# Attention of a hybrid decoder step: ScalarE scales each item's weights by a factor that VectorE makes; GpSimd leaves the attention

## What is computed

```
# q (T, 8 heads, 64), two K/V groups of 4 heads; query block i holds 128 tokens
p_c = masked_softmax(q . kc);  o_c = p_c @ vc                 # 32 compressed blocks
p_s = masked_softmax(q . ks);  o_s = p_s @ vs                 # selected: here all causal keys
p_w = masked_softmax(q . kw);  o_w = p_w @ vw                 # window of 512 tokens
out = g[..., 0:1] * o_c + g[..., 1:2] * o_s + g[..., 2:3] * o_w   # g = sigmoid(gates), per token, head, branch
```

## Time and profile before

| | us |
|---|---|
| median of three runs | 2125.23 (2118.19 to 2125.60) |
| the profiled run | 2124.39 |
| span of its profile | 2122.2 |
| attention in it | about 462 to 850 |

### The profile page before, as it was taken

One profiled execution on the slowest core, in us unless ns is written; L12 is line 12 of the kernel. 1 busy time (PEld: TensorE's weight loads), 2 busy tenths in 40 slices (PEclk: granted clock), 3 DMA queues, 4 the chain that ended last, 5 costly groups with the idle time before them and its releaser, 6 DMA issues.

```text
span 2122.2 us, 28687 instructions
## 1 busy us (share of the span) xinstructions
PE 2029.2 (96%) x11391; PEld 1604.4 (76%) x11391; DVE 810.9 (38%) x1514; ACT 516.8 (24%) x934; POOL 389.5 (18%) x447
## 2 busy tenths in 40 slices
PE   6999999989999998999999998899999999999998
PEld 3588877775666555666676676899999999988875
DVE  2444334466665657422202256311111111235354
ACT  2322100234443444101101045311111111123232
POOL 0000111222231323221000055000000000155542
PEclk8999999989999999999999998999999999999999
DMA  9342010032000000663324354112112112235453
GB/s 362 126 157 100 21 41 21 1 97 70 11 11 11 11 10 3 179 170 108 102 59 129 111 177 139 61 40 60 40 40 60 40 40 60 87 122 168 146 188 104
DMA packets 172940, 184.89 MB, mean 87 GB/s; under 512 B 9893, under 2 KB 143117, under 8 KB 172366
## 3 DMA queue, kind: packets, MB, share of 16 engines
q1 hardware_dynamic: 172814, 183.12, 27.7%
HBM read 170.74 MB, written 16.53 MB: 88 GB/s over the span
## 4 chain that ended last, share of the span: by engine, by line
PE 87%; DVE 4%; DMA 2%; ACT 2%; issue 2%; POOL 1%; SPq 1%; ACTq 0%; POOLq 0%; DVEq 0%
PE ps L2605 23%; PE ps L2507 11%; PE ps L2110 9%; PE ps L2131 5%; PE ps L2549 5%; PE ps L2550 5%; PE ps L2551 5%; PE ps L2377 4%; PE ps L2367 3%; PE ps L2328 3%; PE ps L2345 3%; DMA arena<-in_w_ada 1%; POOL arena L1000 1%; PE ps L2070 1%; DVE arena L601 1%
## 5 line engine op out<-in xcount | busy, mean ns | idle before, releaser
L2605 PE MATMUL ps<-h_hi,wup_hi 128*128 128x344 f32 x1056 | 338.3, 320 | 3.0 <-DVE wup_lo L1978 1.6
L2605 PE MATMUL ps<-h_lo,wup_hi 128*128 128x344 f32 x1056 | 338.9, 321 | 0.0
L2605 PE MATMUL ps<-h_hi,wup_lo 128*128 128x344 f32 x1056 | 338.6, 321 | 0.0
L1031 POOL CAST ra_hi<-arena 128x384 fp32r<-128x384 f32 (+1 forms) x90 | 52.7, 586 | 862.3 <-PE ps L2605 465.7
L2549 PE MATMUL ps<-rw_hi,ra_hi 128*128 128x512 f32 x480 | 193.0, 402 | 13.7 <-DVE rw_lo L1846 13.7
L2605 PEld LDWEIGHTS ps<-h_hi,wup_hi 128*128 128x128 f32 x1056 | 199.3, 189 | 3.4 <-DVE wup_lo L1978 1.9
L2605 PEld LDWEIGHTS ps<-h_lo,wup_hi 128*128 128x128 f32 x1056 | 199.0, 188 | 0.0
L2605 PEld LDWEIGHTS ps<-h_hi,wup_lo 128*128 128x128 f32 x1056 | 198.8, 188 | 0.0
L2110 PE MATMUL ps<-arena,hT 128*128 128x261 f32 (+2 forms) x768 | 194.3, 407 | 3.4 <-ACT hT L1097 2.5
L2550 PE MATMUL ps<-rw_hi,ra_lo 128*128 128x512 f32 x480 | 190.6, 397 | 0.0
L2551 PE MATMUL ps<-rw_lo,ra_hi 128*128 128x512 f32 x480 | 190.0, 396 | 0.0
(11 more groups left out here) (417 smaller groups left out, 2871.3 us busy)
## 6 DMA issues: line engine op xcount, KB each, us to landing
hT<-in_w_down SPq DMA_DIRECT2D x65, 512.0 KB, 3.3
arena<-in_w_ada SPq DMA_DIRECT2D x12, 2048.0 KB, 8.0
arena<-in_w_up SPq DMA_DIRECT2D x44, 512.0 KB, 4.5
arena<-in_w_out SPq DMA_DIRECT2D x24, 512.0 KB, 3.9
arena<-in_w_in SPq DMA_DIRECT2D x19, 512.0 KB, 4.4
arena<-in_cache_cmp_kv SPq DMA_DIRECT2D x64, 128.0 KB, 2.0
arena<-in_cache_slc_kv SPq DMA_DIRECT2D x128, 64.0 KB, 1.9
arena<-in_w_in SPq DMA_DIRECT2D x4, 1544.0 KB, 13.5
```

Source lines behind the costliest of these rows:

```text
L2605: ins = nc.tensor.matmul(ps[:, bank, 0:TG], w[:, k0 + k, :], h[:, k, toks], start=(k == 0 and j == 0), stop=(k == KD - 1 and j == 2))
```

## The change

GpSimd's loop over the items goes. VectorE's `att_rec` makes the reciprocal, waits for its own result (`step`) and multiplies it by the gate column, a 128x1 operation, in place in `rec`; only then it signals `s_rec`. ScalarE gets `att_scale`, an Identity activation over `pbuf` in place, with `rec` as the scale of each partition, which signals `s_scaled`. In iteration n it stands first in ScalarE's queue, for item n + 1, ahead of `take_T(n)`. For compressed items it does nothing. TensorE's code is unchanged.

```diff
@@ block.gpsimd
-            pool.wait_ge(s_gts, 1)
-            for n, (j, k, e) in enumerate(items):
-                if k is None:
-                    continue
-                kind, i, _, nb = span_of(k)
-                u, col = unit_at(n), 3 * (2 * j + e) + 2 - kind
-                pool.wait_ge(s_rec, u + 1)
-                nc.gpsimd.tensor_scalar(pbuf[u % 3][:, 0:nb * P], pbuf[u % 3][:, 0:nb * P], rec[:, u % 4:u % 4 + 1],
-                                        gts[:, i, col:col + 1], ALU.mult, ALU.mult).then_inc(s_scaled, 1)
@@ block.scalar
+            def att_scale(t):
+
+                if items[t][1] is None:
+                    return
+                u, n = unit_at(t), span_of(items[t][1])[3] * P
+                act.wait_ge(s_rec, u + 1)
+                nc.scalar.activation(pbuf[u % 3][:, 0:n], pbuf[u % 3][:, 0:n], ACT.Identity, scale=rec[:, u % 4:u % 4 + 1])\
+                  .then_inc(s_scaled, 1)
+
             for n, (j, k, e) in enumerate(items):
+                if n + 1 < NI:
+                    att_scale(n + 1)
                 take_T(act, nc.scalar.copy, n, 1)
@@ block.vector, att_rec
-                u = unit_at(t)
+                j, k, e = items[t]
+                u, col = unit_at(t), 3 * (2 * j + e) + 2 - span_of(k)[0]
                 dve.wait_ge(s_exp, t + 1)
-                nc.vector.reciprocal(rec[:, u % 4:u % 4 + 1], rsum[:, u % 4:u % 4 + 1]).then_inc(s_rec, 1)
+                step(nc.vector.reciprocal(rec[:, u % 4:u % 4 + 1], rsum[:, u % 4:u % 4 + 1]))
+                nc.vector.tensor_tensor(rec[:, u % 4:u % 4 + 1], rec[:, u % 4:u % 4 + 1], gts[:, span_of(k)[1], col:col + 1], ALU.mult)\
+                  .then_inc(s_rec, 1)
```

## The result

The changed kernel takes 2130.91 us (median of 11 executions, 2130.04 to 2139.61), the kernel before on the same occasion 2125.03 (11 executions, 2117.93 to 2127.87). The medians differ by 5.88 us (0.28%); the ratio on record, taken over all these executions, is 1.0047, 95% interval 1.0033 to 1.0060, which would be 10 us. So the change is slower, by 0.3 to 0.6%. Forecast were 2138.3 us, 13.1 us more, and a range of 2128 to 2150. The forecast gave 0.60 to a time over 0.5% longer: the measured ratio lies just under that line and its interval on both sides of it.

A forecast was written before the change was run, and what follows sets the result against it. TensorE, busy 96% of the span, was taken as the bound, with the chain between transpose groups deciding in the attention. Terms 4.5 + 2.8 + 4.7 + 1.0 + 0.1 = 13.1 us on 2125.2 gave 2138.3 us, range 2128 to 2150.

The forecast's parts named there:

- rival 2: Only head-pair changes and half the mask delay cost, if ScalarE scales 640 columns within 0.74 us: 2131 us; chance 0.27.
- part 1: Chain from reciprocal to scaled weights 0.09 us longer at 50 TensorE waits: 4.5 us (2.7 wide items, 1.8 narrow).
- part 2: VectorE's multiply pushes the next mask and exponential back 0.20 us in 14 narrow items: 2.8 us, between 0 and 4.
- part 3: At three head-pair changes ScalarE's copy waits behind a 1024-column scaling, delaying query transposes 1.57 us each: 4.7 us.
- part 3, tanh: 10 gate products wait for ScalarE's tanh, 0.1 us more each: 1.0 us, between 0 and 2.
- T of the last item: At the attention's end, the last item's transposes find their second bank 0.1 us late: 0.1 us.
- Part 4: GpSimd loses its 128 scalings (100 us busy), but its next work starts no earlier: 0.
- Rival 3: In narrow items ScalarE's ring, 1.83 us against 1.70, sets the pace, costing 0.2 in all 64: 2148 us; chance 0.08.
- Rival 4: Identity with a tensor scale brings two table loads for each of 128 items, over 300 us: 2450 us; chance 0.01.
- Rival 1: TensorE's granted clock falls at all three head-pair changes after added idle time, 7.1 us added: 2145 us; chance 0.15.

The follow-up runs named there:

- experiment 1: Changed kernel, but at the three head-pair changes ScalarE copies its bank of T(n) before scaling item n+1; ratio 1.0027 against the kernel before, +5.5 us at equal clock.
- Experiment 3: Changed kernel, but GpSimd scales by VectorE's factor and, in a second multiply, by ones; ratio 1.0024 against the kernel before, +7.7 us at equal clock.
- 4: Changed kernel without the gate multiply, ScalarE scaling by the reciprocal alone (output differs); ratio 1.0005 against the kernel before, +1.7 us at equal clock.
- 5: Changed kernel with one more dependent 128x1 multiply (by ones) on VectorE behind the factor; 2142.23 us, ratio 1.0094 against the kernel before.
- 6: Changed kernel with ScalarE copying its bank of T(n) before scaling n+1 in every iteration; ratio 1.0032 against the kernel before, +7.0 us at equal clock.
- 7: Kernel before, but GpSimd scales a wide item's first columns and ScalarE the rest, copy first at head-pair changes; 2114.12 us, ratio 0.9956.
- experiment 8: Kernel before, but GpSimd scales each wide item in two instructions and TensorE starts after the first; ratio 1.0016, +3.3 us at equal clock.
- experiments 2: Changed kernel, but GpSimd does the scaling, with one multiply by VectorE's factor, and ScalarE scales nothing; 2195.91 us, ratio 1.0329 against the kernel before.

## Why the prediction was right in kind and too large in size

The number of the first comparison, 2130.91 us, is the 2131 of rival 2 and not the forecast's 2138.3. That is chance: rival 2's mechanism did not happen, as its own test below shows, and the forecast's mechanisms did, at a smaller size. That the time fell into the range owes as much to the range's width (it took in rival 2) as to the sum.

Fixed costs, by the terms of the sum, against what the traces of after show:

| step | forecast, us | measured, us |
|---|---|---|
| part 1, wide items | 2.7 | 1.8 |
| part 1, narrow items | 1.8 | 0.6 |
| part 2, mask pushed back | 2.8 | 2.1 |
| part 3, copy behind the scaling, three changes | 4.7 | 4.9 |
| part 3, tanh | 1.0 | not seen |
| T of the last item | 0.1 | not seen |
| sum | 13.1 | 9.4 |
| at equal clock | | 8.8 (8.0 to 9.6) |

The 4.9 is the time from the first query transpose to the gate products, 2.75, 2.84 and 3.15 us less 1.19, 1.34 and 1.34. (In the second trace of after it is 0.4 us more at the first change, where the second four transposes ran at the low clock, 1.11 us instead of 0.66.) The 2.1 of part 2 are whole steps, of which the longer chain is 0.08 each; in the forecast's own terms part 1 measured 3.0 of 4.5 us and part 2 1.5 of 2.8. The same reckoning, the shift in the items plus that delay, holds for the other kernels too: 4.4 against 5.5 at equal clock for experiment 1, 8.5 against 7.7 for 3, 1.8 against 1.7 for 4, 20.9 against 20.0 for 5, 5.9 against 7.0 for 6, -6.2 against -5.9 for 7. Only experiment 8 is off by more than its interval, 1.7 against 3.3.

**Part 1: the size of one step was right, the count was not.** Forecast were 50 steps of 0.09. The shift, by the starts of the weight loads, has 48 steps of about 0.08 (29 wide, 19 narrow) besides the eight of part 2, but 18 of them are given back at the scores behind: there the weight load waited, and the matmuls ahead of it still ran. I had counted the waits of the load queue (50 times) and taken the rest for cover. The loads overlap the matmuls, so a late load costs only what it leaves the array idle. Left are 30 steps, 2.4 us, and with the eight of part 2 the chain costs in 38 places: fewer than the 50 waits of the loads and more than the 26 of the row of the matmuls.

**Part 2: the mechanism was right, the count again too large.** Eight steps of 0.20 to 0.30, 2.1 us in all, not fourteen. The first is at 486.52, the last at 797.12, the second is that of the example in the text, 591.65 (0.27). The others of the fourteen (483.08, 579.60, 676.96, 680.08, 772.54, 775.66) had a slack that I had looked for on TensorE and not on VectorE. Reciprocal and mask of the load at 676.96, before and after:

```profile
674.88 0.15 DVE L1700 RECIPROCAL arena<-arena 128x1 f32<-128x1 f32 x1
675.05 0.30 DVE L1674 TENSOR_TENSOR ps<-ps,const 128x128 f32<-128x128 f32 x1
```
```profile
676.88 0.15 DVE L1701 RECIPROCAL arena<-arena 128x1 f32<-128x1 f32 x1
677.07 0.16 DVE L1702 TENSOR_TENSOR arena<-arena 128x1 f32<-128x1 f32 x1
677.15 0.29 DVE L1674 TENSOR_TENSOR ps<-ps,const 128x128 f32<-128x128 f32 x1
```

In the eight the mask started 0.07 to 0.08 us behind the reciprocal's start (588.97 and 589.04 in the earlier trace rows) and now starts 0.26 to 0.28 behind it: pushed back by 0.19 or 0.20, as forecast. In the other six it started 0.16 to 0.22 behind, held by the scores, and now starts 0.26 to 0.28 behind: pushed by 0.04 to 0.12 only, which leaves no lasting step over 0.09. Over the whole attention the mask waited for the scores 54 times before the change, 28.5 us in all, and 26 times after it, 12.3 us (the last rows of the two fences of waits above). The text had named this as its lower bound and put a wrong value between the bounds.

**Part 3: the new wait has its place and its size.** 1.57 each forecast, 1.56, 1.50 and 1.81 measured, and experiment 1 takes it away. The tanh's 1.0 us has no place in the shift; its waits went from 10 to 8.

**Part 4** is right as far as seen: nothing that GpSimd's leaving gained or cost shows in the traces, beside steps of 1.6 us and more behind the attention that go with the clock.

**Rival 2** (not slower) fell at its own test: 828 ns, not 740. **Rival 3** fell too: there are eight late masks, not 64 late items, and any two of them are 8 us or more apart, which is several items: no ring on ScalarE sets the pace. Experiment 3, in which ScalarE scales nothing, has the narrow items late too, by 4.0 us. **Rival 4**: one table load in the stretch, as before.

**Rival 1** is wrong in its form. It said that the added idle time would bring the clock down at all three changes, as at the second one before: 0.89, 0.77, 1.00 became 0.89, 0.84, 0.89 in one trace and 0.89, 0.92, 0.89 in the other. Only the third fell. At the second TensorE idled more than before and had the higher clock, and experiment 1, which takes the idle time away, had the lowest of all, 0.79, 0.77, 0.79. The Trainium skill ("TensorE: Matmul & The Clock Gate", Part 1: The HAM clock gate) has idleness throttle the array and activity release it. The third change after agrees (1.00 to 0.89), the second (0.77 to 0.84 or 0.92) and experiment 1 don't by themselves: the added length of idle time doesn't order these rows.

What the clock gave back at the changes, 1.2 us in one trace (4.9 less 3.7) and 3.8 in the other, and what executions differ by otherwise, is of the size of what lies between the 5.9 us of the first comparison and the fixed costs; how much of it each of them made is not shown. The forecast took the kernel before at 2125.2 us, on three executions; that was right for the first occasion (2125.03), while over the 65 later ones its median is 2122.7. Whether the change itself alters how often the clock is low is open: its mean over the executions is 0.9798 before, 0.9789 after, 0.9779 in experiment 1, with 65, 21 and 10 of them. That experiment 1 is no faster in its raw median than after is put down to that clock, which its own edit may or may not bring about; it wasn't settled.

## What to carry to other kernels

To price a longer chain, read the waits of the matmuls beside those of the weight loads: here the loads waited 50 times, the matmuls 26, and the longer chain cost in 38 places. Before charging a small instruction to the queue it stands in, look whether what follows it was waiting for another engine anyway. When an operation moves to another in-order queue, look for the one place where what stands behind it is awaited: here three copies out of 132 cost as much as the longer chain of all 128 items, and one line of order undoes their waits, though the clock kept that gain out of the raw time. Two engines that each do a part of an operation at the same time can beat the better one of them: here the first part needed only the shorter half of the chain.

## What the runs showed of the hardware

- GpSimd's tensor_scalar with one multiply takes 1885 ns for 128x640 fp32 in SBUF, with two multiplies 878 ns: a second operation with a factor of one made the instruction 2.1 times as fast (experiments 2 and 3).
- The mean granted clock of one and the same kernel, before, runs from 0.977 to 0.984 between executions, with 1.57 us of span for 0.001. A comparison of kernels that differ by 5 us does better at equal clock: the medians of after and before lie 5.9 us apart on the first occasion and 10.7 on another; at equal clock, over all, it is 8.8.
- The stretch of 21 us around the attention's first item takes one of two courses, with a clock of 0.67 or 0.84 and 2.3 us between them, and the same kernel, after, took both.
